# Attention by pairs of heads: probabilities normalised before they are turned, values stationary

## The reference

```python
def one_block(qi):
    s = jnp.einsum('bqhgd,bkhd->bhgqk', qi, k, preferred_element_type=jnp.float32) * scale
    p = jax.nn.softmax(s, axis=-1).astype(v.dtype)
    return jnp.einsum('bhgqk,bkhd->bqhgd', p, v)
...
mix = (jax.nn.sigmoid(g_att) * jnp.einsum('bsc,cd->bsd', att, lw['w_att_o']) + ...
```

## Time and profile before

| | us |
|---|---|
| median of 3 runs (lowest, highest) | 2526.43 (2525.85, 2528.55) |
| the profiled execution | 2525.71 |
| its span, first to last instruction | 2523.8 |
| TensorE busy | 2206.0 |
| VectorE busy | 1202.8 |
| ScalarE busy | 812.0 |
| mean granted TensorE clock | 0.939 of 2.4 GHz |

### The profile page before, as it was taken

One profiled execution on the slowest core, in us unless ns is written; L12 is line 12 of the kernel. 1 busy time (PEld: TensorE's weight loads), 2 busy tenths in 40 slices (PEclk: granted clock), 3 DMA queues, 4 the chain that ended last, 5 costly groups with the idle time before them and its releaser, 6 DMA issues.

```text
span 2523.8 us, 25329 instructions
## 1 busy us (share of the span) xinstructions
PE 2206.0 (87%) x10527; PEld 1661.2 (66%) x10527; DVE 1202.8 (48%) x1490; ACT 812.0 (32%) x998; POOL 285.1 (11%) x204
## 2 busy tenths in 40 slices
PE   1999989799999969999659999997999995999991
PEld 0587755488886547777537776646888745777770
DVE  0293244422332378878456523524223244888773
ACT  1123432110000147777332243311000011677761
POOL 2132010100000021111021301002000000111102
PEclk9999999899999879999879998998999995999995
DMA  7224330211124279999631333011211313899974
GB/s 267 85 102 182 134 142 1 100 51 67 60 74 161 98 275 366 372 364 373 226 145 67 136 134 135 9 67 51 78 56 67 128 59 118 320 369 370 366 286 150
DMA packets 114005, 417.13 MB, mean 165 GB/s; under 512 B 7896, under 2 KB 10056, under 8 KB 89184
## 3 DMA queue, kind: packets, MB, share of 16 engines
q1 hardware_dynamic: 89056, 329.27, 35.5%
q0 software_dynamic: 20048, 68.32, 7.5%
q10 hardware_dynamic: 4784, 17.87, 1.7%
HBM read 378.89 MB, written 36.54 MB: 165 GB/s over the span
## 4 chain that ended last, share of the span: by engine, by line
PE 77%; ACT 8%; DVE 7%; DMA 4%; issue 2%; POOL 1%; SPq 0%; ACTq 0%; DVEq 0%; POOLq 0%
PE ps L646 66%; ACT expert_high L1359 4%; PE ps L761 2%; PE ps L657 2%; PE ps L774 2%; DVE x_low L1832 2%; DMA work<-y_dram,slots_u 2%; ACT branch L1394 1%; DMA ring_lo<-in_w_mod_dram 1%; ACT x_high L1364 1%; PE ps L912 1%; PE ps L1037 1%; DVE work L1592 1%; PE ps L762 1%; SPq L449 0%
## 5 line engine op out<-in xcount | busy, mean ns | idle before, releaser
L1826 DVE TENSOR_TENSOR expert_low<-ring_lo,expert_high 128x2048 fp32r<-128x2048 f32 x192 | 436.3, 2289 | 86.8 <-ACT expert_high L1359 80.4
L1359 ACT ACTIVATE expert_high<-ring_lo 128x2048 fp32r<-128x2048 f32 x192 | 364.2, 1913 | 169.4 <-PE ps L646 151.0
L646 PE MATMUL ps<-ring_lo,hT 128*128 128x512 f32 (+1 forms) x800 | 314.8, 552 | 14.0 <-ACT hT L1193 13.9
L646 PEld LDWEIGHTS ps<-ring_lo,hT 128*128 128x128 f32 x800 | 151.2, 191 | 165.7 <-issue 162.0
L646 PE MATMUL ps<-expert_high,x_high 128*128 128x512 f32 x512 | 210.2, 411 | 43.4 <-DVE x_low L1832 43.4
L646 PE MATMUL ps<-branch,ring_lo 128*128 128x320 f32 x768 | 214.4, 432 | 0.0
L646 PE MATMUL ps<-expert_high,x_low 128*128 128x512 f32 x512 | 202.4, 395 | 0.0
L646 PE MATMUL ps<-expert_low,x_high 128*128 128x512 f32 x512 | 201.0, 393 | 0.0
L1308 ACT ACTIVATE work<-ps 128x640 f32<-128x640 f32 x48 | 33.7, 703 | 503.3 <-PE ps L646 503.3
L646 PE MATMUL ps<-h_hi,w_hi 128*128 128x320 f32 x768 | 186.9, 325 | 1.7 <-issue 1.7
L646 PEld LDWEIGHTS ps<-branch,ring_lo 128*128 128x128 f32 x768 | 143.7, 190 | 53.2
(11 more groups left out here) (273 smaller groups left out, 3288.7 us busy)
## 6 DMA issues: line engine op xcount, KB each, us to landing
ring_lo<-in_w_gate_dram SPq DMA_DIRECT2D x64, 1024.0 KB, 8.7
ring_lo<-in_w_up_dram SPq DMA_DIRECT2D x64, 1024.0 KB, 7.2
ring_lo<-in_w_down_dram SPq DMA_DIRECT2D x64, 1024.0 KB, 6.9
ring_lo<-in_w_in_dram SPq DMA_DIRECT2D x26, 2048.0 KB, 7.9
ring_lo<-in_w_mod_dram SPq DMA_DIRECT2D x24, 2048.0 KB, 13.0
y_dram<-branch ACTq DMA_DIRECT2D x32, 512.0 KB, 8.7
ring_lo<-in_w_out_dram SPq DMA_DIRECT2D x4, 2048.0 KB, 8.6
work<-mod_dram POOLq DMA_DIRECT2D x12, 512.0 KB, 6.7
```

What stands on the lines that cost most here:

```text
L646: return pe.matmul(out, lhsT, rhs, start=(k == 0), stop=(k == n - 1))
L1359: A(e_high[n % HIGH], e_raw[n % RAW], ACT.Copy).then_inc(ec_a.sem, 1)
L1826: TT(out=e_low[n % RAW], in0=e_raw[n % RAW], in1=e_high[n % HIGH].bitcast(F32), op=ALU.subtract).then_inc(el_v.sem, 1)
```

## The change

The units are ordered by pairs. Unit u is head `a = u % 2` of pair `v = u // 2`; a pair is the two query heads that lie on the two halves of the partitions in `qT`, one for each key/value head. VectorE now multiplies each unit's probabilities with the reciprocal of their row sum (`norm_probs`) before TensorE turns them, and in its program the row maximum of unit u+1 stands ahead of the normalisation of unit u. `values(v)` makes both heads of a pair at once: stationary are the 64 value columns, moving the 128 columns of `probT`, and the two heads write the upper and the lower 64 partitions of one bank, which are two column strips of the array. The result has channels on partitions already, so `att_out` and `turn_att` go, and ScalarE copies 128x128 a pair to `attT` (20 copies a layer for 5). As the channels come in another order, `w_att_o` is loaded in two halves of 64 partitions. The modulation groups run after the turns of units 14 and 26 (14 and 30 before).

```diff
@@ -46,7 +46,7 @@
-MOD_TURNS = {2: 1, 4: 2}
+MOD_TURNS = {14: 1, 26: 2}
@@ -254,8 +254,9 @@
-            use_of[key], slot_of[key] = uses[s], s
-            uses[s] += 1
+            n = 2 if key[1] == "o0" else 1
+            use_of[key], slot_of[key] = uses[s] + n - 1, s
+            uses[s] += n
@@ -309,11 +310,10 @@
+        nm_v = signal("probs_normed", 40)
         pt_a = signal("probsT_ready", 40)
         pv_p = signal("pv_done", 40)
-        at_v = signal("att_ready", NT)
-        at_p = signal("att_turned", NT)
-        at_a = signal("attT_ready", NT)
+        at_a = signal("attT_ready", 20)
@@ -498,8 +498,15 @@
+                    held[s] = key
+                    if key[1] == "o0":
+                        for a in range(2):
+                            part = slice(a * DH, (a + 1) * DH)
+                            sp.dma_start(slot[s][part, :].rearrange("p (i c) -> p i c", i=4),
+                                         I["w_att_o"][key[0], 4 * DH * a:4 * DH * (a + 1), :].rearrange(
+                                             "(i d) c -> d i c", d=DH)).then_inc(full[s], 16)
+                        continue
                     load(s, *source(key))
-                    held[s] = key
                     continue
@@ -750,13 +757,16 @@
...
                 def score(u):
-                    tt, h = divmod(u, HQ)
-                    half, i4 = divmod(h, 4)
-                    b = 2 * (u % 2)
+
+                    v, a = divmod(u, 2)
+                    tt, i4 = divmod(v, 4)
+                    b = 2 * a
                     if u >= 2:
                         w(pe, e_a, l, u - 1)
-                    part = slice(half * DH, half * DH + DH)
+                    part = slice(a * DH, a * DH + DH)
...
                 def turn_probs(u):
-                    w(pe, e_a, l, u + 1)
+                    w(pe, nm_v, l, u + 1)
                     if u >= 1:
                         w(pe, pt_a, l, u)
-                    nk = 5 if u // HQ < NS else 1
-                    for c in range(nk):
+                    for c in range(5 if u // HQ < NS else 1):
                         out = ps[:, 4, c * P:(c + 1) * P] if c < 4 else ps[:, 5, 0:P]
                         i = pe.transpose(out, prob[u % 2][:, c * P:(c + 1) * P], ident)
                     i.then_inc(pt_p.sem, 1)
-                def values(u):
-                    tt, h = divmod(u, HQ)
-                    kv = 640 + DH * (h // 4)
-                    w(pe, pt_a, l, u + 1)
-                    if h == 0 and tt >= 2:
-                        w(pe, at_a, l, tt - 1)
-                    if h == 0 and tt in MOD_TURNS:
-                        pe.wait_ge(mod_ev, MODT * l + 4 + 4 * MOD_TURNS[tt])
+                def values(v):
+
+                    tt = v // 4
+                    w(pe, pt_a, l, 2 * v + 2)
+                    if v >= 2:
+                        w(pe, at_a, l, v - 1)
+                    if 2 * v in MOD_TURNS:
+                        pe.wait_ge(mod_ev, MODT * l + 4 + 4 * MOD_TURNS[2 * v])
                     nk = 5 if tt < NS else 1
                     for c in range(nk):
-                        if tt == PROMPT:
-                            v = zq[:, PROMPT, kv:kv + DH]
-                        elif c < NS:
-                            v = zq[:, c, kv:kv + DH]
-                        else:
-                            v = v_cache[:, kv - 640:kv - 640 + DH]
-                        i = mm(ps[:, 6 + tt % 2, h * DH:(h + 1) * DH], probT[u % 2][:, c * P:(c + 1) * P], v, c, nk)
-                    i.then_inc(pv_p.sem, 1)
-
-                def turn_att(tt):
-                    w(pe, at_v, l, tt + 1)
-                    for c in range(4):
-                        i = pe.transpose(ps[:, 6 + tt % 2, c * P:(c + 1) * P], zq[:, tt, c * P:(c + 1) * P], ident)
-                    i.then_inc(at_p.sem, 1)
-
-                NU = NT * HQ
+                        for a in range(2):
+                            kv = 640 + DH * a
+                            if tt == PROMPT:
+                                val = zq[:, PROMPT, kv:kv + DH]
+                            elif c < NS:
+                                val = zq[:, c, kv:kv + DH]
+                            else:
+                                val = v_cache[:, kv - 640:kv - 640 + DH]
+                            i = mm(ps[a * DH:(a + 1) * DH, 6 + v % 2, 0:P], val, probT[a][:, c * P:(c + 1) * P], c, nk)
+                            if c == nk - 1:
+                                i.then_inc(pv_p.sem, 1)
+
...
@@ -808,20 +813,15 @@
+                    if u >= 2 and u % 2 == 0:
+                        values(u // 2 - 1)
                     turn_probs(u)
-                    if u >= 1:
-                        values(u - 1)
-                    if u >= 11 and (u - 11) % HQ == 0:
-                        turn_att((u - 11) // HQ)
-                    if u % HQ == 6 and u // HQ + 1 in MOD_TURNS:
-                        tt = u // HQ + 1
-                        w(pe, at_a, l, tt - 1)
-                        mod_group(l, MOD_TURNS[tt], 6 + tt % 2)
-                values(NU - 1)
-                turn_att(NT - 1)
-
-
-                w(pe, e_a, l, NU)
+                    if u in MOD_TURNS:
+                        w(pe, at_a, l, u // 2 - 1)
+                        mod_group(l, MOD_TURNS[u], 6 + (u // 2) % 2)
+                values(NU // 2 - 1)
+
+                w(pe, pv_p, l, NU)
                 for n, (_, tt) in enumerate(STATES):
...
@@ -1246,32 +1245,42 @@
+                NU = NT * HQ
+
                 def exp_unit(u):
                     n = 640 if u // HQ < NS else P
                     w(act, mx_v, l, u + 1)
+                    if u >= 2:
+                        w(act, pt_p, l, u - 1)
                     A(prob[u % 2][:, 0:n], two(2 * (u % 2))[:, 0:n], ACT.Exp, bias=negmax[:, u:u + 1],
                       accum_out=psums[:, u:u + 1]).then_inc(e_a.sem, 1)
 
-                def take_att(tt):
-                    w(act, at_p, l, tt + 1)
-                    w(act, hr_g, l, 2)
-                    A(attT[:, :, tok(tt)], heads(bank(6 + tt % 2)), ACT.Copy).then_inc(at_a.sem, 1)
-
-                NU = NT * HQ
+                def take_probs(u):
+                    n = 640 if u // HQ < NS else P
+                    w(act, pt_p, l, u + 1)
+                    if u >= 2:
+                        w(act, pv_p, l, 2 * (u // 2))
+                    A(probT[u % 2][:, 0:n], two(4)[:, 0:n], ACT.Copy).then_inc(pt_a.sem, 1)
+
+                def take_att(v):
+                    w(act, pv_p, l, 2 * v + 2)
+                    if v == 0:
+                        w(act, hr_g, l, 2)
+                    A(attT[:, v % 4, tok(v // 4)], bank(6 + v % 2, P), ACT.Copy).then_inc(at_a.sem, 1)
+
                 exp_unit(0)
                 take_z(5 * NT - 1)
                 for u in range(NU):
                     if u + 1 < NU:
                         exp_unit(u + 1)
-                    w(act, pt_p, l, u + 1)
-                    n = 640 if u // HQ < NS else P
-                    A(probT[u % 2][:, 0:n], two(4)[:, 0:n], ACT.Copy).then_inc(pt_a.sem, 1)
-                    if u >= 12 and (u - 12) % HQ == 0:
-                        take_att((u - 12) // HQ)
-                    if u % HQ == 7 and u // HQ + 1 in MOD_TURNS:
-                        tt = u // HQ + 1
-                        take_mods(l, MOD_TURNS[tt], 6 + tt % 2)
-                take_att(NT - 1)
+                    take_probs(u)
+                    if u == 5:
+                        take_att(0)
+                    if u >= 5 and u % 2 == 1:
+                        take_att((u - 3) // 2)
+                    if u - 1 in MOD_TURNS:
+                        take_mods(l, MOD_TURNS[u - 1], 6 + ((u - 1) // 2) % 2)
+                take_att(NU // 2 - 1)
@@ -1564,23 +1573,25 @@
-                def att_out(tt):
-                    w(V, pv_p, l, HQ * (tt + 1))
-                    step.do(V.reciprocal(recip[:, HQ * tt:HQ * tt + HQ], psums[:, HQ * tt:HQ * tt + HQ]))
-                    TT(out=zq[:, tt, 0:512].rearrange("p (h d) -> p h d", d=DH),
-                       in0=bank(6 + tt % 2).rearrange("p (h d) -> p h d", d=DH),
-                       in1=recip[:, HQ * tt:HQ * tt + HQ].unsqueeze(2).broadcast_to([P, HQ, DH]),
-                       op=ALU.mult).then_inc(at_v.sem, 1)
-
-                for u in range(NT * HQ):
+                def row_max(u):
+                    n = 640 if u // HQ < NS else P
                     w(V, s_p, l, u + 1)
-                    n = 640 if u // HQ < NS else P
                     V.tensor_reduce(negmax[:, u:u + 1], two(2 * (u % 2))[:, 0:n], AX.X, ALU.max,
                                     negate=True).then_inc(mx_v.sem, 1)
-                    if u >= 9 and (u - 9) % HQ == 0:
-                        att_out((u - 9) // HQ)
-                att_out(NT - 1)
-
+
+                def norm_probs(u):
+                    n = 640 if u // HQ < NS else P
+                    w(V, e_a, l, u + 1)
```

(21 more changed lines are left out.)

## The result

The changed kernel takes 2676.73 us (median of 4 runs, 2669.40 to 2681.34) against 2527.49 us of the kernel before on the same chip (4 runs, 2525.85 to 2529.52): a ratio of 1.0587, with a 95% interval of 1.0558 to 1.0616. It is 149 us slower. The direction was forecast, the size was not: 2594 us was, and the range ended at 2640. One of the six runs of e4_two_ahead (experiment 4) was in a slower state, 2554.96 us at a mean clock of 0.889 against 0.935 to 0.938 in the other five; it is in that kernel's median and not in its ratio.

What follows compares the result with a forecast made beforehand. The prediction took TensorE to bound the attention stage. Wait +42, clock +28, modulation turns +6 and removed work -8 summed to +68 us on 2525.7, giving 2594 us, range 2553 to 2640.

Steps and rivals of the forecast that it cites:

- The order and the wait: Attention units: turns wait for VectorE's row maximum, reciprocal and multiplication, 1.64 us; a pair 7.38 against 6.07 us, +42 us.
- The values: Value products of a pair: two strips overlap, 1.07 us, the gain of 1.06 us a pair hidden beside the wait.
- The clock: Attention stage: one stretch of 3 us per pair at 1.2 GHz, +28 us, with ends of nothing and +97.
- rival 1: Attention stage: the clock holds at 2.4 GHz, 2566 us in all; chance 0.33.
- its own rule: Low stretches in attention pairs lose a share of 1 - 7.38/10.4 of their time; 0.87 us of 3 us.
- The reason given for the fall: Pauses in attention pairs hold only turns, which don't count as busy time for the clock gate as matmuls do.
- Rival 2: TensorE spends the whole attention stage at 1.2 GHz: +141 us, 2667 us in all; chance 0.05.
- The modulation turns: At modulation groups, values wait 3.4 us for evictions after the turns; 1.6 us more, four times: +6 us.
- The prompt's eight units: End of the attention stage: 13.6 us before, then 12 at 2.4 GHz or 15.5 at 1.2; taken as 0.
- What is removed: Attention output turns and the last tile's tail of 2.1 us go; 4 us a layer, -8 us.
- the two small ones: Evictions at the modulation groups, +6 us, and removed attention output turns with the last tile's tail, -8 us.

Runs made afterwards that it cites:

- e4_two_ahead: Changed kernel with scores of unit u+2 made before unit u is turned, all three engines' programs reordered alike; 2510.25 us, 0.9936 of the kernel before.
- e1_fill: Changed kernel with matmuls whose result nobody reads filling TensorE's wait before the turns; 2594.48 us, 1.0280 of the kernel before.
- e10_more_turns: Changed kernel with the wait filled by unread turns alone, 11 in odd units and 3 in even ones; 2596.20 us, 1.0283 of the kernel before.
- e2_norm_first: Changed kernel with VectorE normalising unit u ahead of the row maximum of u+1; 2547.29 us, 1.0075 of the kernel before.
- e9_fill_turns: Changed kernel with the wait filled in part by unread turns, six in odd units; 2611.24 us, 1.0327 of the kernel before.
- e3_one_column: Changed kernel with the normalising multiplication on one column in place of 640; 2641.09 us, 1.0464 of the kernel before.

## Why the prediction was wrong

The order and the wait were right, and one term of the sum, the clock's, was mis-sized by a factor of nearly four. By the prediction's own steps:

- **The order and the wait: right.** Every odd steady unit has row maximum, reciprocal and multiplication on the chain between scores and turns; in the even ones the values stand there at 1.2 GHz, as the prediction said they would. The multiplication takes 0.55 to 0.56 us, as estimated between the earlier trace rows. A pair at 2.4 GHz takes 7.23 us (e1_fill) instead of 7.38: 32 x (7.23 - 6.07) = 37 us for the forecast 42.
- **The values: right.** Two strips side by side, 1.24 us for the forecast 1.07 (e4_two_ahead), hidden under the wait where the clock is high and on the chain where it is low. Where the other 0.17 comes from, no run shows.
- **The clock: the step that failed.** "I choose one low stretch per pair, as long as the row of 510 to 513, 3 us" made +28. Three of some 8.25 us would be 36% of the time at 1.2 GHz; it was 68% and 70%, in low stretches of some 7 to 20 us. The 3 us came from a row behind whose fall TensorE ran without a pause (3.00 busy of 3.00 us), while every pair now has further pauses behind a fall. The trace of before held a nearer row, in its prompt units, where TensorE pauses for 0.41 and 1.02 us:

```profile
333.00:340.00 7.00, 5.52 (x21) 4.08 (x20) 1.77 (x5) 2.64 (x11) 2.04 (x2) 0.50 1.06 388
```

The prediction used that fall against rival 1 and for the growth of the narrow scores, not for its length. With 7 us a pair its own rule gives 32 x 7 x (1 - 7.38/10.4) = 65 us for the 28, an estimate, and a sum of 2631. And a pair at 1.2 GHz is 11.35 us, not 10.4: turns 2.59 where the sum had 2.0, scores 4.87 for 4.6, values 2.33 for 2.14, the wait 1.56 for 1.68. Worked out again from these rows, as an estimate: 0.68 x 208 = 141 us a layer at 1.2 GHz, of which 1 - 7.23/11.35 = 36% are lost, 51 us; 0.70 x 208.7 = 146 us and 53 us in layer 1. Together 104 us for the forecast 28, past the upper end of 97 that the prediction had named. Filling the pause alone gives back 82 of it (e1_fill), with the clock not yet at 1.00 there.
- **The reason given for the fall: half right.** The prediction took the pauses with "only turns between them" at 506 us as a sign that turns don't hold the clock. The pauses were the reason and the turns were not: a pause filled with turns alone holds it as one filled with multiplications does (e10_more_turns 1.0283, e1_fill 1.0280). The rule cited there, that of the Trainium skill's page "TensorE: Matmul & The Clock Gate", section "Part 4: PE-mode transpose", by which turns don't count as busy time as matmuls do, is not borne out by these runs.
- **Rival 2, the whole stage at 1.2 GHz, 2667 us,** had been given 5% and lies 10 us from the measured time. That is luck: its share of low time was too high (all of the stage for 68% and 70%), and its pair was too short (10.4 us for 11.35). The argument against it, that TensorE is busy most of a pair at that clock (9.78 of 11.35 us here), did not keep low stretches from lasting up to 20 us, 1.8 pairs, though the clock came back between them. The range stopped at 2640 and left this case out, though the end of its price was written in the sum.
- **The modulation turns: right in mechanism.** The values start 3.3 us after the turns end (305.93 to 309.26), for the forecast 3.4.
- **The prompt's eight units:** put at 0, with 2 us either way a layer. They took 18.0 us (396.07 to 414.08) for 13.6, at a clock of 0.68; what the clock has in this lies in the 104 us above.
- **What is removed: right.** The values end at 414.82 and the next stage starts at 414.87.
- **Not foreseen:** the multiplication that is held by GpSimd's additions, 3.77 + 0.95 us instead of 1.1 in layer 0 and 3.76 + 0.95 in layer 1, 3.6 us each. The additions stood in the trace of before at the same place (213.75 us, 11.15 us); the prediction listed what is queued behind the new instruction on VectorE and didn't look at GpSimd beside it.

The sum with the measured terms, and the two small ones as forecast: 37 + 104 + 6 - 8, and 7 for the held multiplications, is +146 us, against 149 measured. That it comes so close is in part chance: the 104 us hold some 3 to 4 us a layer that the kernel before lost too (its clock averaged 0.97 and 0.96 over the two stretches).

## What to carry to other kernels

When a change puts a wait into every turn of a loop that TensorE bounds, price the turn at both clocks and take the lower clock as a case for the whole loop; the lost clock can cost more than twice the wait itself. An engine that runs in order makes its next unit's first step part of this unit's last one: working two units ahead on all three engines at once took the wait away, and only then did the cheaper products show, while moving one engine alone left a shorter wait at the next one (e2_norm_first, 0.46 us a pair). Before a VectorE instruction between two places of SBUF is added, look at what GpSimd runs at that time.

## What the runs showed of the hardware

- A pause of 1.56 us in a pair of units, filled with multiplications or with turns that nobody reads, moved the mean granted clock of a stretch from 0.68 to 0.94 (206 to 330 us). Stretches of steady pairs with a pause of 0.46 us (e2_norm_first, 238 to 276 us) or 0.77 (e9_fill_turns, 297 to 342) kept 1.00; with pauses of 1.22 (e3_one_column) and 1.56 us the clock swung between its levels, 0.72 and 0.68 on average.
- A VectorE multiplication of 128x640 (0.55 us alone) that meets a GpSimd addition ends 0.35 us after that addition's end, and took up to 4.95 us; row maxima (0.82) and reciprocals (0.15) beside it kept their times.
- Twenty passes of 128 columns with 64 stationary columns took 2.33 us in one strip, 1.95 in two strips one head after the other, 1.24 in two strips that alternate.
